# Two blocks of a hybrid network on one core: where ScalarE issues the reciprocal row's fetch and store in the first attention

## The reference, cut to what matters

```python
def forgetting_attention(q, k, v, log_f):
    s, d = q.shape[1], q.shape[-1]
    scale = d ** -0.5
    cum = jnp.cumsum(log_f, axis=1).transpose(0, 2, 1)
    for i in range(s // Q_BLOCK):
        q0, q1 = i * Q_BLOCK, (i + 1) * Q_BLOCK
        logits = jnp.einsum('bqhd,bkhd->bhqk', q[:, q0:q1], k[:, :q1]) * scale
        logits = logits + (cum[:, :, q0:q1, None] - cum[:, :, None, :q1])
        logits = jnp.where(mask, logits, -jnp.inf)
        probs = jax.nn.softmax(logits, axis=-1)
        outs.append(jnp.einsum('bhqk,bkhd->bqhd', probs, v[:, :q1]))
```

## Time and profile before

| | us |
|---|---|
| median of 3 executions | 1438.65 |
| lowest and highest | 1436.66, 1438.85 |
| the profiled execution, its own time | 1433.96 |
| span of its trace | 1432.2 |
| PE busy in the span | 1370.6 (96%) |
| DVE busy | 698.0 (49%) |
| ACT busy | 547.4 (38%) |
| POOL busy | 688.3 (48%) |

### The profile page before, as it was taken

The page is one execution under the profiler, slowest core; times in us unless marked ns, Lnnn a source line. Parts: engine busy times, 40 slices in busy tenths (PEclk is TensorE's granted clock), DMA queues, the critical chain, the costliest instruction groups (busy, mean ns, idle before and its releaser), DMA issues.

```text
span 1432.2 us, 17281 instructions
## 1 busy us (share of the span) xinstructions
PE 1370.6 (96%) x6567; PEld 1124.0 (78%) x6567; DVE 698.0 (49%) x1005; ACT 547.4 (38%) x793; POOL 688.3 (48%) x544
## 2 busy tenths in 40 slices
PE   2999999999999999999999998999999999999999
PEld 2887787778777878888888886886788888888887
DVE  6676978788843672141324456357623213132231
ACT  0635454476662262141332316324525223132231
POOL 0453855332346655445445544753644445445442
PEclk9999999999999999999999999999999999999999
DMA  9353445755323432322232232342122332232232
GB/s 331 116 136 93 98 129 173 207 142 150 104 59 130 146 92 88 109 96 88 88 117 88 88 110 72 105 120 77 45 93 89 105 101 88 92 102 99 88 98 78
DMA packets 132249, 158.58 MB, mean 111 GB/s; under 512 B 9469, under 2 KB 93713, under 8 KB 131937
## 3 DMA queue, kind: packets, MB, share of 16 engines
q1 hardware_dynamic: 123760, 146.95, 32.6%
q10 hardware_dynamic: 6240, 5.40, 1.7%
q0 software_dynamic: 2192, 5.49, 1.2%
HBM read 153.47 MB, written 2.26 MB: 109 GB/s over the span
## 4 chain that ended last, share of the span: by engine, by line
PE 81%; DVE 9%; POOL 3%; issue 2%; ACT 2%; DMA 1%; SPq 0%; ACTq 0%; DVEq 0%; POOLq 0%
PE bank L1702 25%; PE bank L1703 24%; PE bank L1704 24%; DVE tmp L1268 3%; POOL w_lo L546 3%; PE bank L1839 1%; DMA arena<-in_w_ada_dram 1%; DVE rinv L1175 1%; PE bank L1970 1%; PE bank L2208 1%; PE bank L1824 1%; ACT w_hi L740 1%; PE bank L1849 1%; PE bank L2026 1%; PE bank L1852 1%
## 5 line engine op out<-in xcount | busy, mean ns | idle before, releaser
L546 POOL TENSOR_TENSOR w_lo<-raw,w_hi 128x512 fp32r<-128x512 f32 x428 | 585.2, 1399 | 605.9 <-ACT w_hi L740 604.7
L1702 PE MATMUL bank<-w_hi,a_hi 128*128 128x512 f32 x928 | 365.3, 394 | 13.3 <-POOL w_lo L546 6.5
L1703 PE MATMUL bank<-w_lo,a_hi 128*128 128x512 f32 x928 | 362.6, 391 | 0.0
L1704 PE MATMUL bank<-w_hi,a_lo 128*128 128x512 f32 x928 | 362.6, 391 | 0.0
L740 ACT ACTIVATE w_hi<-raw 128x2048 fp32r<-128x2048 f32 x107 | 204.7, 1913 | 356.8 <-PE bank L1704 353.6
L1702 PE MATMUL bank<-a_hi,w_hi 128*128 128x512 f32 x800 | 315.7, 395 | 3.4 <-DVE a_lo L1161 2.5
L1703 PE MATMUL bank<-a_lo,w_hi 128*128 128x512 f32 x800 | 312.2, 390 | 0.0
L1704 PE MATMUL bank<-a_hi,w_lo 128*128 128x512 f32 x800 | 312.0, 390 | 0.0
L1702 PEld LDWEIGHTS bank<-w_hi,a_hi 128*128 128x128 f32 x928 | 175.1, 189 | 51.7 <-DVE a_lo L1161 6.2
L1704 PEld LDWEIGHTS bank<-w_hi,a_lo 128*128 128x128 f32 x928 | 175.0, 189 | 36.9
L1703 PEld LDWEIGHTS bank<-w_lo,a_hi 128*128 128x128 f32 x928 | 175.1, 189 | 35.7
(11 more groups left out here) (248 smaller groups left out, 1258.6 us busy)
## 6 DMA issues: line engine op xcount, KB each, us to landing
raw<-in_w_mlp_dram SPq DMA_DIRECT2D x32, 1024.0 KB, 5.3
raw<-in_w_in_dram SPq DMA_DIRECT2D x24, 1024.0 KB, 5.2
arena<-in_w_ada_dram SPq DMA_DIRECT2D x18, 1024.0 KB, 6.5
raw<-in_w_ff_in_dram SPq DMA_DIRECT2D x16, 1024.0 KB, 5.4
raw<-in_w_ff_out_dram SPq DMA_DIRECT2D x16, 1024.0 KB, 5.1
raw<-in_w_out_dram SPq DMA_DIRECT2D x12, 1024.0 KB, 5.6
raw<-in_w_in_dram SPq DMA_DIRECT2D x16, 512.0 KB, 5.7
arena<-in_w_ada_dram SPq DMA_DIRECT2D x3, 2048.0 KB, 18.1
```

Source lines behind the costliest of these rows:

```text
L546: last = pool.tensor_tensor(w_lo[:, u0 % 2, cols], raw[:, u0 % 2, cols], w_hi[:, u0 % 2, cols].bitcast(F32), ALU.subtract)
L1702: pe.matmul(out_, hi_a, hi_b, start=start, stop=False)
L1703: pe.matmul(out_, hi_a, lo_b, start=False, stop=False)
L1704: return pe.matmul(out_, lo_a, hi_b, start=False, stop=stop)
```

## The change

In ACT's program of the first attention, three pieces of a step change places. Before, the order was: fetch (s-2), copies (s-2), exponentials (s-1), in even steps the rounding of a weight unit, store (s-1). Now it is: copies, exponentials, fetch, store, rounding. No instruction is added or removed, and no other engine's program changes.

```diff
                 if s >= 2:
-                    fetch_inverse(s - 2)
                     copy_probT(s - 2, probT)
                 if 1 <= s < 17:
                     probabilities(s - 1, score, prob)
+                if s >= 2:
+                    fetch_inverse(s - 2)
+                if 1 <= s < 17:
+                    send_inverse(s - 1)
                 if s % 2 == 0 and 2 <= s < 14:
                     hi(U_QK1 + s // 2)
                 elif s == 17:
                     hi(U_WO1 + 2, late=1)
-                if 1 <= s < 17:
-                    send_inverse(s - 1)
                 if s == 14:
```

## The result

| us | before | after |
|---|---|---|
| median of five executions | 1438.65 | 1428.14 |
| lowest | 1434.16 | 1426.99 |
| the profiled execution, its own time | 1433.96 | 1426.99 |
| span of its trace | 1432.2 | 1425.3 |
| step 2 to step 17, start to start of PE's transposes | 148.33 | 142.77 |

The changed kernel is faster: the ratio is 0.9933, with a 95% interval from 0.9916 to 0.9951. It is a difference of two starts, so nothing before the stage enters it.

What follows compares the result with a forecast made beforehand. PE is 96% busy, so only about 5.9 us of its gaps in the first attention could be won. Terms 1.15 + 1.08 + 1.8 - 0.4 = 3.6 give 1430.4 profiled, 1435.0 median; range 1432.5 to 1441.0.

Steps and rivals of the forecast that it cites:

- the same difference gives: Step from profiled execution to median: before's 4.7 us difference added to 1430.4, giving 1435.0.
- Step 2: ACT's copies no longer wait behind head 0's fetch; reciprocal some 2.4 us earlier, 1.15 plus 1.08 us of PE waits gone.
- The weighing out of POOL's way: Steps 7 and 11: later rounding starts POOL after DVE's weighing, so PE waits of 0.26 and 1.53 go, 1.8 us.
- The sum: First attention: 1.15 + 1.08 + 1.8 - 0.4 = 3.6 us won against the profiled execution.
- 1.15, 1.08 and 1.8: PE waits won: 1.15 for copies and exponentials, 1.08 for output in steps 3 and 4, 1.8 in steps 7 and 11.
- I take 0.4 us lost: DVE's `mxs`, held by POOL's later pieces, mainly in steps 9 and 13: 0.4 us lost in all.
- The waits of 0.8 ... stay.: End of stage: PE waits of 0.8 (lo part, step 14), 0.4 and 0.7 us stay, their orders being unchanged.
- the wait of 0.7: PE's wait for the unit after step 17's output, claimed to stay at 0.7 us.
- The fetch in odd steps: Issued 0.8 us after the first exponential; in step 7 lands 1.6 us before the output needs it, nothing lost.
- The slow rival: Odd steps 3 to 13: fetch falls behind the weight load and lands late, 6.6 us lost, time 1441.7; chance 0.18.
- The rule of turns between queues: DMA engines alternate queues by packet, so a fetch behind a load is served early: rival's price near nothing, time 1435.
- No difference: DVE stays the pace: step 10's weighing still held, or `mxs` held in two or three steps; 1437.5 us, chance 0.34.

Runs made afterwards that it cites:

- the step-2 kernels: Against before, only step 2's fetch moved behind the exponentials: median 1432.98 us, ratio 0.9972; with the rounding behind the store as well: 1430.01, ratio 0.9963.
- step 2 only: Against before, the fetch moved behind the exponentials in step 2 alone: median 1432.98 us, ratio 0.9972, stage 147.35 us.
- fetches only: Against before, all fetches moved behind copies and exponentials, rounding still ahead of the store: median 1434.12 us, ratio 0.9983, stage 147.28 us.
- before again: The kernel before, unchanged, run again: median 1435.79 us of 12 runs (1432.69 to 1441.64), stage 147.54 us.
- the changed kernel again: The changed kernel, unchanged, run again beside before: median 1428.89 us of 12 runs, ratio 0.9966, stage 142.78 us.
- rounding only: Against before, only the rounding moved behind the store, fetches still ahead of the copies: median 1431.16 us, ratio 0.9955, stage 145.21 us.
- the last kernel: Changed kernel with step 17's rounding ahead of that step's copies and exponentials, run beside the changed kernel: median 1429.61 us against 1430.85, stage 144.15 us.

## Why the prediction was right or wrong

**How far off, and by what.** The forecast of 1435.0 lies 6.9 us above the median of 1428.14. The sum for the stage was 2.0 us too small. Another 1.4 us lie outside the stage (1.6 for the half-speed stretch, less 0.3 lost in step 18). And 3.5 us are the step from the profiled execution to the median: "the same difference gives" took the 4.7 us of before over to after, where the median lies only 1.2 us above the profiled execution. That step is what put the result outside the range; with the stage's 5.56 us alone the forecast would have been 1433.1, inside it.

**Step 2, right.** Copies at 270.04, exponentials at 273.26, reciprocal at 275.49, against 270.3, 273.4 and 275.6. That it is this fetch and no other is shown by the step-2 kernels.

**The weighing out of POOL's way, right.** Steps 7 and 11 run at full pace as soon as the rounding stands behind the store, with or without the fetches. The Trainium skill (SBUF — State Buffer, Who interferes with whom) says that a DVE instruction with two SBUF inputs contends with a POOL instruction that reads SBUF, and the one that issued first makes the other wait. By that rule the trace agrees: 4.02 us with POOL beside it, 2.02 without.

**The sum, too small: 3.6 against 5.56.** The mechanism was right, and the sum failed in three of its terms.
- *The price of each stop.* I took the idle times of the rows. A stop costs PE 0.1 to 0.2 us more than its row says: 1.15, 1.08 and 1.8 came out as 1.30, 1.51 and 2.22 us (steps 2, 3 and 4, 7 and 11), 1.0 us over six stops, 0.1 to 0.2 each. The end of a matmul is modelled: one lasts 0.39 us in the rows, while the next starts 0.23 us behind it, so the idle time is counted from an end that is late. The start of an instruction to the next start gives the whole.
- *"I take 0.4 us lost" for `mxs`.* In steps 9 and 13 it took 0.57 and 0.57 us before and 0.17 after. The holds went to steps 7 and 11 (0.42 and 0.43), where DVE has slack, and the one of step 3 shrank from 1.15 to 0.55, so nothing was lost: 0.4 us more.
- *"The waits of 0.8 ... stay."* The 0.8 us wait of step 14 for DVE's lo part fell to 0.5, and 0.4 us were won in step 14. It was the tail of the `mxs` hold in step 13, one step upstream, from which DVE runs on without a pause to that lo part: the four traces with the early rounding have `mxs` there at 0.47 or 0.57 us and step 14 at 10.92 to 11.73, the eight with the late rounding and the fetch ahead of the store 0.17 us and 10.50 to 10.55. Another 0.1 us came in step 10. Behind the stage the wait of 0.7 did not stay either. Its order was changed, by the fetch that now stands ahead of step 17's rounding, and it grew to 1.0.

1.0 + 0.4 + 0.5 = 1.9, and 3.6 + 1.9 = 5.5.

**The fetch in odd steps, right in its outcome and wrong in its timing.** I took its issue as 0.8 us after the first exponential, "when half are done"; it was 0.08 us. The row at 310.41 had the rule: the fetch goes once the last wait ahead of it is over, however many activations have still to run. Here that is the wait for `mxs`, and the fetch left 0.1 us behind it in even steps, where ACT was still copying, as in odd ones. The eight instructions ahead of it cost nothing. The Trainium skill (Perfetto Trace Analysis, DVE / Act Engine Instruction) has an activation wait in a queue of its own while the sequencer goes on to the next instruction. By that the fetch would have left before `mxs` was written; the traces disagree, in none of the 77 cases did it. The program writes this wait as a statement of its own ahead of the exponentials, and whether that makes the difference no run shows.

**The slow rival, alive but kept out.** A fetch issued together with a load landed after 5.1 to 6.1 us, as it had to by its row. In the changed kernel the load left 1.1 us behind the fetch, since the late rounding delays it. Moving the fetches alone, which takes that delay away, gave late landings and part of that loss, and one trace of the changed order had them twice without a price. The rule of turns between queues (the Trainium skill, DMA: Bandwidth & Descriptors, Queues, rings and completion order) would have made that landing little longer than the 2.7 us of a fetch alone (an estimate); the measurement decides against it here.

**No difference, wrong.** Its condition, that the weighing stays held, is what "step 2 only" and "fetches only" show; the changed kernel has none of it.

**The range, too narrow at the fast end, and partly bad luck.** Its best case of 5.0 us adds up to 4.8 from its own terms (1.15 + 1.08 + 1.8 + 0.8), and I ended it a us below for the "spread of the runs". Of the 10.5 us between the first medians the stage explains 5.6. The profiled executions lie 7.0 us apart, 1.6 of them the half-speed stretch near 455 us. The other 3.5 us are in how each kernel's runs are spread, and were not the same again: medians of before were 1436.49, 1438.97 and 1434.73 in the three groups, with 7.6 and 3.9 us between it and the changed kernel beside it. Of all runs, the lowest of before is 1432.2 and the lowest of after 1426.99, 5.2 us apart. Had the first medians stood in the ratios of the later groups (0.9966 and 0.9972), 1438.65 would have become 1433.8 or 1434.6, inside the range: so the miss of the range is owed to the draw of the first runs at least as much as to the 2.0 us missing in the sum.

## What to carry to other kernels

When ACT's program holds a DMA that waits for a landing, everything behind it waits too: put what others wait for ahead of it, and check only the step in which the landing is late. Here that was one of sixteen. A DMA queued behind computing instructions leaves when the last wait ahead of it is over, so count the waits ahead of it and not the instructions. A transfer's place matters less than what is issued beside it, so look which load a moved instruction sets free, and when. Two gains that meet in a shared resource are to be tried together as well as apart: alone the first was mostly given back at the second, together they kept both. And price a PE stop from start to start, and a median from the spread of more than three runs.

## What the runs showed of the hardware that was not expected

- **Runs of one kernel fall mostly into two groups, 5 us and more apart, by granted clock.** The runs of both kernels split by granted clock: before again had seven runs from 1432.69 to 1436.56 at 0.993 to 0.995 and five from 1438.72 to 1441.64 at 0.990 to 0.991; the changed kernel again had eight from 1428.08 to 1429.80 at 0.994 to 0.995 and four from 1435.33 to 1438.26 at 0.988 to 0.990. One profiled execution shows where: "fetches only" (profiled at 1438.42 us) ran at 1.2 GHz in two stretches ahead of the stage, near 190 and 254 us, where the profiled execution of after did not, and its stage begins 6.8 us later (275.43 against 268.62). Its windows, third figure from the right:
```profile
188.00:192.00 4.00, 3.51 (x23) 3.54 (x24) 0.35 (x1) 1.98 (x3) 4.00 (x4) 0.75 0.10 8
192.00:196.00 4.00, 4.00 (x16) 3.61 (x16) 1.78 (x3) 0.00 (x0) 3.61 (x3) 0.50 0.74 254
252.00:256.00 4.00, 3.86 (x9) 3.12 (x10) 3.63 (x8) 0.00 (x0) 1.49 (x3) 0.50 0.70 194
```
  The code there is the same in all kernels. What brings a run into the one group or the other stays open.
- **After a stop of 1.85 us PE fell to half speed in some traces and not in others.** Near 450 us both traces of before and "rounding only" did (0.57 to 0.68 in one window), the changed kernel's three traces did not, but neither did "step 2 only" and "fetches only". It cost 1.6 us in the first trace of before and is not explained by the edits.
- **A 128 KB fetch issued 0.1 to 1.7 us behind a 1 MB load took 4.3 to 6.9 us,** although the two stand in different queues: 5.1 to 6.1 in "fetches only", 5.1 to 5.9 in the first trace of before, 4.3 and 4.5 in the last kernel, and 6.9 in step 3 of "step 2 only". Issued 1.1 to 1.2 us ahead of the load it took 2.7 to 3.4 in the first trace of after.
- **Activations ahead of a DMA in ACT's program did not delay it, their wait did.** The fetch left 0.1 us after `mxs`, with at least the last seven of the exponentials' eight instructions still to run.
